# Expert tokens picked as rows by long products and transposed, in every pair; the token table in device memory given up

## The reference, cut to what matters

```
g_w, g_idx = top_k(softmax(x @ w_group + b_group), 1)          # one of 4 groups
e_w, e_idx = top_k(softmax(logits of that group), 2)           # two of its 4 experts
h = silu(einsum('nd,edf->nef', xt, w_gate)) * einsum('nd,edf->nef', xt, w_up)
y = einsum('nef,efd->nd', h * combine[:, :, None], w_down)     # 16 experts, d_ff = 512
```

## Time and profile before

| what | us |
|---|---|
| median of 3 runs | 1168.8 |
| the profiled execution | 1168.16 |
| its span | 1166.3 |
| PE busy | 1105.4 (95%) |
| DVE busy | 414.0 (36%) |
| ACT busy | 229.2 (20%) |
| POOL busy | 128.3 (11%) |

### The profile page before, as it was taken

The page is one execution under the profiler, slowest core; times in us unless marked ns, Lnnn a source line. Parts: engine busy times, 40 slices in busy tenths (PEclk is TensorE's granted clock), DMA queues, the critical chain, the costliest instruction groups (busy, mean ns, idle before and its releaser), DMA issues.

```text
span 1166.3 us, 19793 instructions
## 1 busy us (share of the span) xinstructions
PE 1105.4 (95%) x8488; PEld 654.0 (56%) x8488; DVE 414.0 (36%) x1059; ACT 229.2 (20%) x531; POOL 128.3 (11%) x226
## 2 busy tenths in 40 slices
PE   4999999999899999999998899998999899999996
PEld 1666666666444576666654444444555656666562
DVE  2155656556712341000112655306863320000114
ACT  3111011011211321111111411115642411111110
POOL 0344434334100000000002000000000000000003
PEclk9999999999999999999999899999999999999999
DMA  9985444446842579999999920079770789999996
GB/s 346 291 292 149 136 146 146 146 146 217 338 187 89 180 270 423 411 428 427 424 427 348 368 102 1 18 258 371 263 281 18 253 353 418 429 426 424 425 418 227
DMA packets 102464, 321.27 MB, mean 275 GB/s; under 512 B 4048, under 2 KB 39168, under 8 KB 87008
## 3 DMA queue, kind: packets, MB, share of 16 engines
q1 hardware_dynamic: 93872, 298.05, 66.9%
q0 software_dynamic: 3248, 10.87, 2.8%
q10 hardware_dynamic: 5248, 10.98, 2.4%
HBM read 305.73 MB, written 14.16 MB: 274 GB/s over the span
## 4 chain that ended last, share of the span: by engine, by line
PE 80%; DMA 11%; DVE 4%; SPq 2%; issue 2%; ACT 1%; POOL 1%; POOLq 0%; ACTq 0%; DVEq 0%
PE bank L788 17%; PE bank L941 11%; PE bank L1181 11%; PE bank L811 7%; PE bank L678 7%; PE bank L777 6%; DMA ring<-in_moe_w_down 5%; PE bank L950 4%; PE bank L1067 4%; DMA ring<-in_w_ada 4%; PE bank L573 3%; PE bank L966 2%; PE bank L657 1%; DMA ring<-expert_rows,moe_row 1%; PE bank L664 1%
## 5 line engine op out<-in xcount | busy, mean ns | idle before, releaser
L788 PE MATMUL bank<-ring,xn 128*64 128x256 f32 x1472 | 163.5, 380 | 0.9 <-DMA ring<-in_moe_w_up 0.9
L788 PEld LDWEIGHTS bank<-ring,xn 128*64 128x64 f32 x1472 | 105.0, 137 | 61.4 <-issue 9.5
L941 PE MATMUL bank<-uT,ring 128*128 128x384 f32 x384 | 135.0, 496 | 0.0
L1181 PE MATMUL bank<-ring,uT 128*128 128x512 f32 x288 | 129.5, 603 | 4.3 <-DMA ring<-in_attn_w_qkv 2.7
L1869 DVE TENSOR_TENSOR moe_hh<-xn,bank 128x256 f32<-128x256 f32 x32 | 13.5, 421 | 291.7 <-ACT xn L1336 291.6
L811 PE MATMUL bank<-ring,xn 128*64 128x512 f32 x384 | 106.7, 596 | 0.9 <-ACT xn L1342 0.9
L941 PEld LDWEIGHTS bank<-uT,ring 128*128 128x128 f32 x384 | 69.2, 190 | 41.4 <-issue 1.1
L1181 PEld LDWEIGHTS bank<-ring,uT 128*128 128x128 f32 x288 | 54.1, 193 | 68.2 <-issue 64.1
L678 PE MATMUL bank<-ring,uT 128*128 128x512 f32 x192 | 84.1, 592 | 0.0
L777 PE MATMUL bank<-moe_g,moe_h 128*128 128x128 f32 x672 | 83.7, 282 | 0.5 <-DVE moe_g L1759 0.5
L777 PEld LDWEIGHTS bank<-moe_g,moe_h 128*128 128x128 f32 x672 | 79.9, 197 | 5.6 <-issue 5.6
(11 more groups left out here) (293 smaller groups left out, 1328.2 us busy)
## 6 DMA issues: line engine op xcount, KB each, us to landing
ring<-in_w_ada SPq DMA_DIRECT2D x24, 2048.0 KB, 12.1
ring<-in_moe_w_up SPq DMA_DIRECT2D x24, 2048.0 KB, 18.7
ring<-in_moe_w_gate SPq DMA_DIRECT2D x22, 2048.0 KB, 19.5
ring<-in_moe_w_down SPq DMA_DIRECT2D x21, 2048.0 KB, 19.9
ring<-in_hgrn_w_in SPq DMA_DIRECT2D x32, 512.0 KB, 6.9
moe_ring<-in_moe_w_gate SPq DMA_DIRECT2D x8, 2048.0 KB, 19.5
moe_ring<-in_moe_w_up SPq DMA_DIRECT2D x8, 2048.0 KB, 23.3
moe_ring<-in_moe_w_down SPq DMA_DIRECT2D x7, 2048.0 KB, 21.0
```

Of the source, the lines that this page charges most:

```text
L788: last = mm(bank[2 + e][64 * g:64 * g + 64, 256 * part:256 * part + 256], m["xe"][:, k, 64 * e:64 * e + 64], w[k][:, 256 * g:256 * g + 256 ...
L941: last = mm(to[:, 0:TOK], w[:, k, f, :], uT[:, k, :], start=(k == 0), stop=(k == KC - 1))
L1181: last = mm(bank[b % 2][:, :], uT[:, k, t * P:(t + 1) * P], cols(slot)[:, k, :], start=(k == 0), stop=(k == KC - 1))
```

## The change

The gather of every pair, pair 1 too, goes in two steps. `pick_rows` makes the rows of the slots: for each half of the features three products with 128 x 128 of `g` as the stationary operand and 512 columns of `h` as the moving one. ACT and DVE copy banks 0 and 1 to `own` (`picked`). Then `gather` transposes them in 4 blocks for each half, as pair 1's were before, and `rows` copies to `xe`. The picks stand earlier in the pair: half 0 behind `gate_up` of expert 0, half 1 behind the gate part of expert 1. The transposes stand where the gathers were. The store of the token table, the token sums, the integer copy and the indirect load go. DVE's order puts `picked` behind the hidden product of expert 0 and, in pair 6, ahead of the last two gate operands.

```
-FETCHED = 1
+FETCHED = 0
...
+                def pick_rows(half, i):
+                    if half == 0:
+                        pe.wait_ge(s["onehot"], onehots_made(at_pass[0], i))
+                    for t in range(T):
+                        last = mm(bank[half][:, :], m["g"][:, t, :, :], m["h"][:, t, 512 * half:512 * half + 512],
+                                  start=(t == 0), stop=(t == T - 1))
+                    last.then_inc(s["gathered"], 1)
...
+                def gather(half, i, it):
+                    if not fetched(i):
+                        pe.wait_ge((s["xe_act"], s["xe_dve"])[half], it * 2 + 1)
...
                     for k in range(4):
-                        ...
-                        for t in range(T):
-                            last = mm(bank[half][:, k * P:(k + 1) * P],
-                                      m["h"][:, t, (4 * half + k) * P:(4 * half + k + 1) * P],
-                                      m["g"][:, t, :, :], start=(t == 0), stop=(t == T - 1))
+                        here = slice((4 * half + k) * P, (4 * half + k + 1) * P)
+                        last = nc.tensor.transpose(bank[half][:, k * P:(k + 1) * P], m["own"][:, 1, here], ident)
...
                     gate_up(i, 0, 1, it)
+                    if picking:
+                        pick_rows(0, i + 1)
                     if gating:
                         gate(n, m["diag"], 1, 1, 6)
...
                     gate_up(i, 1, 0, it)
+                    if picking:
+                        pick_rows(1, i + 1)
                     if gating:
                         gate(n, m["diag"], 1, 2, 6)
                     gate_up(i, 1, 1, it)
                     if not last:
-                        gather(0, i + 1)
+                        gather(0, i + 1, it + 1)
...
                 def before(p):
-                    gather(0, 0)
-                    tokens_of(1)
-                    gather(1, 0)
+                    pick_rows(0, 0)
+                    pick_rows(1, 0)
+                    gather(0, 0, p * PAIRS)
+                    gather(1, 0, p * PAIRS)
...
+                def picked(i):          # ACT; DVE's is the same for half 1 and bank 1
+                    act.wait_ge(s["gathered"], rows_picked(at_pass[0], i, 0))
+                    A(m["own"][:, 1, 0:512], bank[0][:, :], ACT.Copy).then_inc(s["xe_act"], 1)
...
                         v.tensor_tensor(m["hh"][:, e, :], m["sg"][:, e, :], bank[2 + e][:, 256:512], ALU.mult)\
                             .then_inc(s["h_ready"], 1)
+                        if e == 0 and not last and not fetched(i + 1):
+                            picked(i + 1)
...
-                store_tokens()
-                fetch(0)
```

More of the change, by code:

```diff
@@ L381, in onehots_made, with fetched, gathers_before, rows_picked @@
             return p * ONEHOTS + (i + 1 + min(max(i - 1, 0), FETCHED))
[L383 to L389, removed]
+        def fetched(i):
+            return 1 <= i <= FETCHED
+        def gathers_before(i):
+            return 0 if i == 0 else 4 * i + FETCHED if i == 1 else 4 * i - FETCHED
+        def rows_picked(p, i, half):
+            return p * GATHERS + (gathers_before(i) + half + 1)
         def pair_gathered(p, i, half):
-            return p * GATHERS + (2 * i + half + 1 + (FETCHED if i or half else 0))
+            return p * GATHERS + (gathers_before(i) + (0 if fetched(i) else 2) + half + 1
+                                  + (FETCHED if i == 0 and half == 1 else 0))
         def passes(eng, n):
@@ L754, in weights_in @@
                     return [cols(slot)[:, k, :] for k in range(KC)]
-                def tokens_of(i):
-                    pe.wait_ge(s["onehot"], onehots_made(at_pass[0], i))
+                def pick_rows(half, i):
+                    if half == 0:
+                        pe.wait_ge(s["onehot"], onehots_made(at_pass[0], i))
                     for t in range(T):
-                        last = mm(bank[4][:, 0:1], m["gw"][:, t, :, :], const("token")[:, t:t + 1],
+                        last = mm(bank[half][:, :], m["g"][:, t, :, :], m["h"][:, t, 512 * half:512 * half + 512],
                                   start=(t == 0), stop=(t == T - 1))
                     last.then_inc(s["gathered"], 1)
[L764 to L770, removed]
-                    for k in range(4):
[L772 to L775, removed]
-                        for t in range(T):
-                            last = mm(bank[half][:, k * P:(k + 1) * P],
-                                      m["h"][:, t, (4 * half + k) * P:(4 * half + k + 1) * P],
-                                      m["g"][:, t, :, :], start=(t == 0), stop=(t == T - 1))
+                def gather(half, i, it):
+                    if not fetched(i):
+                        pe.wait_ge((s["xe_act"], s["xe_dve"])[half], it * 2 + 1)
+                    elif half == 0:
+                        pe.wait_ge(s[f"rows{i}"], at_pass[0] * ROWS_IN[i] + 16)
+                    for k in range(4):
+                        here = slice((4 * half + k) * P, (4 * half + k + 1) * P)
+                        last = nc.tensor.transpose(bank[half][:, k * P:(k + 1) * P], m["own"][:, 1, here], ident)
                     last.then_inc(s["gathered"], 1)
@@ L843, in body @@
                 def body(i, it, first, last):
-                    pe.wait_ge(s["xe_act"], it + 1)
+                    pe.wait_ge(s["xe_act"], it * 2 + 2)
+                    picking = not last and not fetched(i + 1)
                     gating = i == GATE_PAIR and isinstance(it, int)
@@ L876, in body @@
                     if not last:
-                        gather(1, i + 1)
+                        gather(1, i + 1, it + 1)
                     pe.wait_ge(s["hT_ready"], it + 1)
@@ L1316, in rows @@
                     act.wait_ge(s["gathered"], pair_gathered(at_pass[0], i, 0))
-                    A(m["xe"][:, 0:4, :], bank[0][:, :], ACT.Copy).then_inc(s["xe_act"], 1)
+                    A(m["xe"][:, 0:4, :], bank[0][:, :], ACT.Copy).then_inc(s["xe_act"], 2 if fetched(i) else 1)
+                def picked(i):
+                    act.wait_ge(s["gathered"], rows_picked(at_pass[0], i, 0))
+                    A(m["own"][:, 1, 0:512], bank[0][:, :], ACT.Copy).then_inc(s["xe_act"], 1)
                 at_pass = [0]
@@ L1322, in before @@
                     at_pass[0] = p
+                    picked(0)
                     rows(0)
@@ L1815, in rows_of_pass, with picked @@
                     then(v.tensor_copy(flat["row"], flat["rowf"]))
-                def tokens_of(i):
-                    dve.wait_ge(s["gathered"], tokens_summed(at_pass[0], i))
-                    v.tensor_copy(m["idx"][:, i - 1:i], bank[4][:, 0:1]).then_inc(s["onehot"], 1)
                 def rows(i):
                     dve.wait_ge(s["gathered"], pair_gathered(at_pass[0], i, 1))
-                    v.tensor_copy(m["xe"][:, 4:8, :], bank[1][:, :].rearrange("p (k n) -> p k n", k=4)).then_inc(s["xe_dve"], 1)
+                    v.tensor_copy(m["xe"][:, 4:8, :], bank[1][:, :].rearrange("p (k n) -> p k n", k=4))\
+                        .then_inc(s["xe_dve"], 2 if fetched(i) else 1)
+                def picked(i):
+                    dve.wait_ge(s["gathered"], rows_picked(at_pass[0], i, 1))
+                    v.tensor_copy(m["own"][:, 1, 512:1024], bank[1][:, :]).then_inc(s["xe_dve"], 1)
                 at_pass = [0]
@@ L2273, in experts @@
                 table = expert_rows[n].rearrange("e c d -> (e c) d")
[L2275 to L2290, removed]
                 def collect(p):
                     pool.wait_ge(s["oe_out"], p * (16 * WRITES) + 16 * WRITES)
-                    pool.wait_ge(s["down_half"], p * 32 + 32)
+                    if isinstance(p, int):
+                        pool.wait_ge(s["down_half"], p * 32 + 32)
+                    else:
+                        pool.wait_ge(*expert_used(n, PAIRS - 1, 5, p))
                     g.tensor_tensor(m["flag"][:, 1:2], ones[:, 0:1], ones[:, 0:1], ALU.mult)
```

15 lines of the change are left out of this document (6 added, 9 removed).

## The result

The changed kernel takes 1206.45 us (median of 4 runs, 1205.30 to 1213.12) against 1168.59 for the kernel before in the same session (4 runs, 1168.21 to 1170.16). The ratio is 1.0333, 95% interval 1.0294 to 1.0372: slower by 37.9 us, where 28.6 were predicted. Direction and mechanism came out as forecast; the size is off by 9 us, which puts the time 0.45 us above the predicted range. The profiled execution took 1206.04 us.

The account below looks back on a forecast made before the run. TensorE was taken to bound the expert stage. Start 0.4, pair 0 5.15, pairs 1 to 5 7.65 and pair 6 2.45 sum to 15.65 us a layer; after absorption 14.1 + 14.5 = 28.6 on 1168.16 gives 1197, range 1186 to 1206.

Parts of the forecast that it names:

- What bounds the kernel: Expert stage: TensorE bounds pairs 0 to 6, added work delays it one for one; weights hide under a microsecond.
- rival of the hidden stream: Expert stage: the weight stream hides the pairs' added work; only start and pair 0 count, 11 us, 1179; chance 0.05.
- The price of a pick: Each pair's 12 pick instructions cost 0.429 us each, 5.15 us, against 5.56 for the old gather.
- Long products are cheap: A layer's 96 pick instructions cost about 0.222 us or less each; 4 us faster in all, 1164; chance 0.07.
- The new handoff: Last gate/up to first down product: 2.41 us in place of 6.03, including waits for DVE and ACT.
- Pair 6: Plus 2.45 us a layer, including a new 1.45 us TensorE wait for DVE's gate operands behind its copy.
- The start: Start of the expert stage: 7.9 us against 7.53, plus 0.4, with 1.29 us of slow clock in both.
- The ends of the layers: Vanishing waits and slack absorb 1.56 us in layer 0 and 1.12 in layer 1; layer 0's QKV load stays hidden.
- The table: Pair 0 without table: handoff stays, the removed load was hidden, picks for pair 1 add 5.15 us, the largest term.
- the edits on GpSimd and DVE: Removing table store, load, waits, one-hots and integer copy: gain bounded by 0 and 1 us a layer, taken as 0.
- The clock falls: In the changed handoffs more transposes and short waits lower TensorE's clock: 15 us slower still, 1212; chance 0.05.

Follow-up runs that it names:

- experiments 1 and 2: Changed kernel with both picks moved: behind the pair's last gate/up product (1179.19 us), or behind the up part of expert 0 (1209.31 us).
- experiment 6: Changed kernel with DVE making pair 6's last two gate operands ahead of its copy of the picked rows: 1211.00 us, ratio 1.0352; on another chip 1212.91 us.
- Experiment 1: Changed kernel with both picks moved behind the pair's last gate/up product, ahead of the hidden transposes: 1179.19 us, ratio 1.0088 to the kernel before.
- experiment 9: Kernel before with long picks for pair 0 alone, at the start of the expert stage: 1172.20 us against 1170.38, ratio 1.0012.
- experiment 4: Changed kernel with the token table and pair 1's indirect load kept, long picks in all other pairs: 1200.15 us, ratio 1.028 to the kernel before.

## Why the prediction came out as it did

- **What bounds the kernel: right.** TensorE's additions came through one for one, and no wait for weights appeared in pair 7. The rival of the hidden stream needed 11 us; 37.9 came.
- **The price of a pick: the step that failed.** "So the picks cost 12 x 0.429 = 5.15 us against 5.56" is right for twelve in a row: 5.35 in experiments 1 and 2, 0.2 of it the way in. In the changed kernel they stand in two groups of six among 64-wide products, and each place costs a further 0.35 us. The twelve cost 5.87. In pair 0 that is 0.70 of the 0.70 missed (5.85 − 5.15), in each of pairs 1 to 5 0.72 of 0.79. That makes 0.70 + 5 x 0.72 = 4.3 a layer, 8.6 us in all, of a miss of 9.3. In pair 6 gate products stood at such places before and paid for them; its 0.22 is the wait for DVE, priced at 1.45 and worth 1.66. With it and the 0.07 that down takes longer in pairs 1 to 5 the pairs missed 9.7. That the total missed about the same is luck: the start came out 1.1 and 0.6 us under the forecast, and the ends and the low clock outside the layers 1.1 over it.
- **It could have been read from the rows.** The earlier trace rows has the two half gathers of a pair at 2.88 and 2.68 us, 24 equal products each; the first stands behind gate/up products, the second behind transposes. The chain of pair 6 before has it as well: gate products (L657) at 1.05 among gate/up products, and 3.60 for the 32 behind them against 3.45. In the prediction the 2.88 and 2.68 were only summed. This is its fragment:

```profile
578.46 3.45 PE bank L788 x32
581.91 1.05 PE bank L657 x2
582.97 3.60 PE bank L788 x32
```

  The Trainium skill has the rule (TensorEngine Tiling (Array Packing), "Key Properties"): changing the tiling mode, and not merely the tile, drains TensorE. It gives no price; the runs agree with it at 0.35 us for going from 64-wide tiles to the full width and back. That it is a drain is the page's reading; the traces show the time lost on either side, and that the first load there doesn't overlap the products before it.
- **Long products are cheap: refuted.** An instruction is 0.429 us in a row ((5.35 − 0.20) / 12), 3.7 times the gather's 0.116. The Trainium skill's figures (TensorE: Matmul & The Clock Gate, "Back-to-back issue gap"), on which that rival leaned beside L811, don't describe these float32 products.
- **The new handoff: right.** Predicted 2.41, measured 2.40, with both waits. Experiment 1 shows what they are worth, 0.98 us a pair once picks stand there.
- **Pair 6: right.** Predicted +2.45, measured +2.67; the wait was named with its cause, and experiment 6 removes it; what it missed was the time that the gate product loses behind the wait.
- **The start: sign wrong, by the clock.** Predicted +0.4 with 1.29 us of slow clock; measured −0.70 in layer 0 (6.83) and −0.18 in layer 1 (7.36). In layer 0 the twelve picks ran in 5.40 us at the full clock; in experiment 9 the clock was 0.77 there and they took 6.96. The 1.29 was read against a half gather behind gate/up products (2.88); against the 2.79 of the second half at the same spot the slow clock cost 1.38. Where the low clock falls isn't in the kernel's text.
- **The ends of the layers: a small miss.** In layer 0 1.56 us were to be absorbed; pair 7 gave back 1.08, and the QKV load was hidden as predicted: the first QKV product no longer waits for it. The other 0.7 was not seen, and 0.4 came on top. In layer 1 the forecast was 1.12, and 1.25 was absorbed.
- **The table: pair 0 is the largest single term, as forecast:** 5.85, by the ledger and by experiment 4. That the edits on GpSimd and DVE cost or gain nothing by themselves fits the periods, but the totals, with their spread, can't show it.
- **The clock falls: not in the pairs.** The mean is 0.991 before, 0.990 after. One pair with its transposes:

```profile
444.22:473.41 29.19, 28.52 (x184) 14.70 (x184) 2.83 (x8) 3.76 (x7) 0.00 (x0) 1.00 0.88 354
```

  The clock is 1.00 over the pair (the third number from the end), in which 12 transposes stand. Over measurements of the changed kernel it went from 0.982 to 0.990 without any change of the program.

## What to carry to other kernels

Price an inserted product by its shape and by its neighbours: among products of another stationary width it costs its own time plus the way in and out, so take the row of the same shape in the same neighbourhood, and put such products together. When work is moved out of a handoff, its cover goes with it: moving the picks back bought 1.57 us a pair, 0.98 of it cover and 0.52 places. Compare steps by periods in the chain, not by total times, where executions of one kernel differ by more than the step is worth.

## What the runs showed of the hardware

- Going from 64-wide stationary tiles to full-width float32 products and back costs 0.35 us with six or twelve picks: 0.20 on the way in, 0.15 to 0.17 over the products behind. With a product of one column it is 0.27 to 0.35. The first stationary load on either side begins only with its product (458.14 and 460.92).
- Two 64-wide one-column products in the same spot cost 0.11 us together, one full-width one 0.46.
- The changed kernel, unaltered, took 1206.45, 1216.22 and 1205.36 us in three measurements, with mean granted clocks of 0.990, 0.982 and 0.990 in the profiles. (1 − clock) x span gives 12, 22 and 12 us of lost clock.
- ACT's SiLU of expert 1 in pair 7 came 2.2 to 3.1 us late in some measurements, released by something the trace can't name. What it waited for is open.
